# A first gated net with four plain tiles, quarter sums on POOL, and rotary angles moved to that net's last stretch

## The reference

```python
D_MODEL = 1024; SEQ = 512; DEPTH = 2; D_FF = 2816

def swiglu(h, w_gate, w_up, w_down):
    return (jax.nn.silu(h @ w_gate) * (h @ w_up)) @ w_down

def first_block(x, ...):
    for l in range(DEPTH):
        x = x + 0.5 * swiglu(rms_norm(x, ffn1_norm[l]), ffn1_wg[l], ffn1_wu[l], ffn1_wd[l])
        ...
        x = x + 0.5 * swiglu(rms_norm(x, ffn2_norm[l]), ffn2_wg[l], ffn2_wu[l], ffn2_wd[l])
    return rms_norm(x, final_norm)

def rope_tables(positions):
    half = QK_ROPE // 2
    inv_freq = ROPE_THETA ** (-jnp.arange(half, dtype=jnp.float32) / half)
    ang = positions.astype(jnp.float32)[..., None] * inv_freq
    return jnp.cos(ang), jnp.sin(ang)
```

## Time and profile before

| | before |
|---|---|
| median of 3 runs | 2509.74 us |
| the profiled execution | 2509.46 us |
| its span (first to last instruction) | 2507.7 us |
| around the span | 1.8 us |
| PE busy | 2492.7 us, 99% of the span |
| DVE busy | 1959.6 us, 78% |
| ACT busy | 1229.5 us, 49% |
| POOL busy | 305.2 us, 12% |
| granted TensorE clock | 1.00 (2.4 GHz) over the span |

### The profile page before, as it was taken

One profiled execution on the slowest core, in us unless ns is written; L12 is line 12 of the kernel. 1 busy time (PEld: TensorE's weight loads), 2 busy tenths in 40 slices (PEclk: granted clock), 3 DMA queues, 4 the chain that ended last, 5 costly groups with the idle time before them and its releaser, 6 DMA issues.

```text
span 2507.7 us, 37031 instructions
## 1 busy us (share of the span) xinstructions
PE 2492.7 (99%) x14550; PEld 2204.2 (88%) x14550; DVE 1959.6 (78%) x2788; ACT 1229.5 (49%) x1957; POOL 305.2 (12%) x250
## 2 busy tenths in 40 slices
PE   8999999999999999999999999999999999999998
PEld 7999988889999889999888899998888888899997
DVE  7878867778888688887777888876899786876663
ACT  6444444444444454444553544445577535644442
POOL 4000001320000000000023100000186221200002
PEclk9999999999999999999999999999999999999999
DMA  5333342223333423333323233334333333233331
GB/s 157 99 97 101 98 107 83 82 87 99 95 110 100 118 79 104 96 108 112 101 65 96 74 101 107 101 106 136 88 72 82 123 92 113 83 108 99 99 100 59
DMA packets 487299, 246.87 MB, mean 98 GB/s; under 512 B 42321, under 2 KB 483926, under 8 KB 486870
## 3 DMA queue, kind: packets, MB, share of 16 engines
q1 hardware_dynamic: 486674, 244.19, 33.9%
q10 hardware_dynamic: 452, 0.32, 0.1%
HBM read 240.27 MB, written 4.19 MB: 97 GB/s over the span
## 4 chain that ended last, share of the span: by engine, by line
PE 95%; DVE 3%; ACT 1%; issue 0%; DMA 0%; POOL 0%; DVEq 0%
PE bank L878 8%; PE bank L877 8%; PE bank L876 8%; PE bank L764 6%; PE bank L766 6%; PE bank L765 6%; PE psS L898 4%; PE psS L899 4%; PE psS L900 4%; PE psT L942 2%; PE psT L943 2%; PE psT L944 2%; PE psT L764 2%; PE psT L766 2%; PE psT L765 2%; PE bank L1441 1%
## 5 line engine op out<-in xcount | busy, mean ns | idle before, releaser
L2238 DVE TENSOR_TENSOR wlo<-raw,whi 128x1024 fp32r<-128x1024 f32 (+2 forms) x212 | 289.3, 1366 | 51.6 <-ACT whi L1567 48.4
L764 PE MATMUL bank<-xhi,whi 128*128 128x512 f32 x672 | 265.3, 395 | 0.0
L765 PE MATMUL bank<-xlo,whi 128*128 128x512 f32 x672 | 261.9, 390 | 0.0
L766 PE MATMUL bank<-xhi,wlo 128*128 128x512 f32 x672 | 261.8, 390 | 0.0
L876 PE MATMUL bank<-xsh,whi 128*128 128x256 f32 x840 | 237.8, 283 | 0.0
L877 PE MATMUL bank<-xsl,whi 128*128 128x256 f32 x840 | 237.7, 283 | 0.0
L878 PE MATMUL bank<-xsh,wlo 128*128 128x256 f32 x840 | 237.7, 283 | 0.0
L1567 ACT ACTIVATE whi<-raw 128x1024 fp32r<-128x1024 f32 (+2 forms) x209 | 214.5, 1030 | 46.0 <-PE bank L766 22.5
L2297 DVE TENSOR_TENSOR wlo<-tw,whi 128x1024 fp32r<-128x1024 f32 x140 | 171.6, 1225 | 62.2 <-ACT whi L1603 62.0
L898 PE MATMUL psS<-hhi,whi 128*128 128x512 f32 x488 | 191.7, 393 | 0.0
L899 PE MATMUL psS<-hlo,whi 128*128 128x512 f32 x488 | 191.6, 393 | 0.0
(11 more groups left out here) (701 smaller groups left out, 7275.0 us busy)
## 6 DMA issues: line engine op xcount, KB each, us to landing
raw<-in_ffn_wg SPq DMA_DIRECT2D x88, 512.0 KB
raw<-in_ffn_wu SPq DMA_DIRECT2D x88, 512.0 KB
raw<-in_w_in SPq DMA_DIRECT2D x53, 512.0 KB
raw<-in_w_mlp SPq DMA_DIRECT2D x40, 512.0 KB
raw<-in_ffn_wd SPq DMA_DIRECT2D x48, 256.0 KB
raw<-in_ffn_wd SPq DMA_DIRECT2D x24, 448.0 KB
raw<-in_ffn_wd SPq DMA_DIRECT2D x48, 192.0 KB
raw<-in_ffn_wd SPq DMA_DIRECT2D x48, 128.0 KB
```

The source lines that it names most:

```text
L764: pe.matmul(dest, a, rhs_hi(k), start=start and k == 0, stop=False)
L765: pe.matmul(dest, a, rhs_lo(k), start=False, stop=False)
L766: mm = pe.matmul(dest, b_, rhs_hi(k), start=False, stop=stop and k == tiles - 1)
L2238: dve.tensor_tensor(wlo[:, a:a + n], raw[:, a:a + n], whi[:, a:a + n].bitcast(F32), ALU.subtract).then_inc(s_split, 1)
```

## The change

Net 0 gets two pairs like the other nets: four plain tiles, 18 windows, another cut of the down-projection. In net 0 the quarter sums are taken from DVE's queue and written into POOL's, where the angles stood; there each group waits for ACT's copies and for the low half of the group before. DVE's low half of the quarter sums stands in net 0 after the SiLU product of its tile and no longer ahead of the up product. The angles follow behind the sums on POOL, from the moment at which the last stretch of net 0 has added its first tile to `x`; they use `inv6` and `first_inv` as scratch, and the wait for them ahead of weight sums stands in net 1.

```diff
-    PLAINS = (3, 2, 2, 2)
+    PLAINS = (2, 2, 2, 2)
...
                 def weight_sums(j):
                     c, g = c0 + 4 * (PLAIN + j), G0 + j
                     landing(c + 1)
-                    if j == 0:
+                    if j == 0 and nf == 1:
                         dve.wait_ge(s_ro, 13)
...
                 def quarter_sums(i):
+                    if nf == 0:
+                        return
...
-                        if 2 * j + p in QUARTERS_AT:
+                        if nf and 2 * j + p in QUARTERS_AT:
                             quarters_lo(QUARTERS_AT[2 * j + p])
                         dve.wait_ge(s_used, c + 2 * p + 2)
                         dve.tensor_tensor(tmp[2 + p][:, :], b(up_b[p][:, :]), inv[:, :], ALU.mult).then_inc(s_us, 1)
                         dve.wait_ge(s_us, f + p + 1)
                         dve.wait_ge(s_si, f + p + 1)
                         dve.tensor_tensor(tmp[2 + p][:, :], tmp[2 + p][:, :], tmp[p][:, :], ALU.mult).then_inc(s_h, 1)
+                        if not nf and 2 * j + p in QUARTERS_AT:
+                            quarters_lo(QUARTERS_AT[2 * j + p])
...
-            r, n = rope[64:128, :], sqt[64:128, :]
+            near, far, half = xg2[:, 0:S], xg2[:, S:2 * S], (slice(0, QT), slice(QT, S))
+            s1, s2, s3, s4 = (xsum[:, j * QT:(j + 1) * QT] for j in range(4))
+            for i in range(4):
+                pool.wait_ge(k_xg, i + 1)
+                if i:
+                    pool.wait_ge(k_xl, i)
+                pool.tensor_tensor(s1, near[:, half[1]], far[:, half[1]], ALU.add).then_inc(k_xs, 1)
+                pool.tensor_tensor(s3, near[:, half[0]], near[:, half[1]], ALU.subtract).then_inc(k_xs, 1)
+                pool.wait_ge(k_xs, 4 * i + 1)
+                pool.tensor_tensor(s2, s1, near[:, half[0]], ALU.subtract).then_inc(k_xs, 1)
+                pool.wait_ge(k_xs, 4 * i + 3)
+                pool.tensor_tensor(s4, far[:, half[0]], s2, ALU.subtract).then_inc(k_xs, 1)
+            r, n, part_r = rope[64:128, :], inv6[64:128, :], first_inv[64:128, :]
...
-            pool.wait_ge(s_inv, 1)
+            pool.wait_ge(s_x, KC + 1)
...
-                pool.tensor_scalar(acc[64:128, :], n, -cst, None, ALU.mult).then_inc(s_ro, 1)
+                pool.tensor_scalar(part_r, n, -cst, None, ALU.mult).then_inc(s_ro, 1)
```

More of the change, by code:

```diff
@@ L3275, in _ @@
                 pool.wait_ge(s_ro, step)
-                pool.tensor_scalar(acc[64:128, :], n, -cst, None, ALU.mult).then_inc(s_ro, 1)
+                pool.tensor_scalar(part_r, n, -cst, None, ALU.mult).then_inc(s_ro, 1)
                 pool.wait_ge(s_ro, step + 1)
-                pool.tensor_tensor(r, r, acc[64:128, :], ALU.add).then_inc(s_ro, 1)
+                pool.tensor_tensor(r, r, part_r, ALU.add).then_inc(s_ro, 1)
                 step += 2
@@ L3281, in _ @@
             pool.tensor_scalar(r, r, 3.1415925, -3.1415925, ALU.min, ALU.max).then_inc(s_ro, 1)
-            c, nn = rope[64:96, :], sqt[64:96, :]
+            c, nn = rope[64:96, :], inv6[64:96, :]
             pool.wait_ge(s_ro, 10)
```

## The result

| | before | after |
|---|---|---|
| median of 15 runs each | 2509.66 us | 2514.59 us |
| the profiled execution | 2509.46 us | 2514.59 us |
| its span | 2507.7 us | 2512.7 us |

What follows compares the result with a forecast made beforehand. PE, busy 99% of the span, was taken as the bound, so only its work or stops count. -1.53 (work) + 4.8 (stop) + 0 (angles) = +3.3 us on 2509.74 gave 2513.0 us, range 2509.4 to 2515.0.

Steps and rivals of the forecast that it cites:

- the forecast proper: Whole kernel: 2513.0 us, band 2511.9 to 2514.5, given a chance of 0.62.
- less work on PE: Net 0: two plain tiles go, 21.76 us, against 20.23 us for more fast tiles and the down-projection's other cut; -1.53 us.
- start of the first window: Net 0's first window would start at 57.50 instead of 79.26, since two plain tiles go.
- walk of DVE without meetings: Plain tiles of net 0: DVE's fourth low half ends at 61.6, PE wants it at 60.4; a stop of 1.2 us.
- meetings of POOL and DVE: Plain tiles of net 0: POOL's sums and DVE's two-SBUF operations hold each other up, adding 3.6 us to the stop.
- both together: the stop: PE's stop at the third product of net 0's first window: 1.2 + 3.6 = 4.8 us (3.7 to 5.7), paid once.
- angles in the last stretch: Net 0's last stretch: the angles on POOL cost 0, at most 0.6 us, as DVE has spare time each round.
- A sum of 0.74: Price of one 256-column quarter sum on POOL: 0.74 us, between 0.65 and 0.83.
- The places of the meetings: Norm's last step, a unit of weights, corner weights through weight sums, last corner's rest: 1.5, 0.5, 1.3 and 0.3 us.
- under 0.9 a round: Net 0's last stretch: the angles hold DVE less than the 0.9 us it has to spare in each round.
- the slower rival: Net 0's last stretch: angles hold DVE for whole rows, rounds grow to about 6, PE loses some 5 us; 2518; chance 0.09.
- The up product and the SiLU product, now ahead of the low half: DVE's walk in net 0's plain tiles: having them ahead of the low half makes 1.3 us of the 1.2 us stop.

Runs made afterwards that it cites:

- fills: Changed kernel with each net 0 quarter sum on POOL replaced by a constant fill that reads nothing, leaving those sums out; 2509.31 us.
- the filled run: Changed kernel with 18 extra matmuls of 512 columns on PE, results unread, ahead of the third product of net 0's first window; 2512.94 us.
- the angles alone: Kernel before with only the rotary angles moved on POOL to net 0's last stretch; three pairs and sums on DVE as before; 2513.28 us.
- sums on DVE: Changed kernel with net 0's quarter sums on DVE instead of POOL, each group behind DVE's own low half of the group before; 2512.90 us.
- low half first: Changed kernel with the quarter sums' low half back ahead of the up product in all four tiles of net 0; 2520.51 us.
- three edits: Changed kernel with down-projection's first share before the third product, fourth group's sums on DVE, last tile's low half before up product, corner rest behind SiLU product; 2514.81 us.
- side first: Changed kernel with the down-projection's first share (9 matmuls) moved ahead of the third product of net 0's first window; 2514.25 us, in two groups.
- fourth group on DVE: Changed kernel with the fourth group of quarter sums on DVE and, in the last plain tile, their low half ahead of the up product; 2512.52 us.

## Why the prediction was right, and where it was short

It put the time at 2513.0 and the sign right; 1.6 us were missing. The median lies 0.09 above the band that was the forecast proper (to 2514.5), and inside the range because that went on to 2515.0. By the profile's steps the changed kernel's loss is:

| step of the prediction | forecast, us | measured, us |
|---|---|---|
| less work on PE | -1.53 | first window to stage behind 308.28; without stop and clock 302.27, net 1 has 302.28 |
| start of the first window | 57.50 | 57.69, +0.19 |
| walk of DVE without meetings | +1.2 | 0.87 with fills, which are shorter than sums |
| meetings of POOL and DVE | +3.6 | 3.55 between fills and sums, at most 0.4 of it length |
| both together: the stop | +4.8 | 4.47 |
| angles in the last stretch | 0 | no stop between units; some 0.2 at the stage behind |
| TensorE's clock behind the stop | not named | +1.54 by rows, 1.65 by the filled run |

-1.53 + 0.19 + 4.47 + 0.2 + 1.54 = 4.9, the measured 4.93. The 0.19 is there ahead of the plain tiles already (DVE's row at 25.00 before is at 25.18 after); no run shows why. The 0.2 lies where the stage behind net 0 waits for the last halves of its input; before has no such wait, and each kernel with the late angles has one (0.17 with fills, 0.8 with the angles alone).

- **The gain and the stop** were read rightly. Third product "near 65": 65.02. A sum of 0.74: 0.73 to 0.75 where nothing meets it. The places of the meetings are the four that were named, and the sizes 1.5, 0.5, 1.3 and 0.3 measured 1.25, 0.42, 1.35 and 0.53.
- **The step that was missing** is in the sum: a stop was priced at its length, with no term and no rival for the clock behind it. The prediction read PE's speed from a kernel whose PE does not rest from 36 to 85 us, and so took 0.12 us a matmul also for what follows a rest of 4.5.
- **The angles**: the answer of 0 was nearly right, but by luck. The hold "under 0.9 a round" was 0.9 to 1.9 us in three rounds, because three of the four additions met a two-SBUF operation of DVE and held it 0.9 to 1.1 us each; a scalar operation held 0.3 to 0.4 (at 346.05 and 353.97), near the 0.5 that was taken. The rounds grew to 5.7, nearly the 6 of the slower rival. What saved the stretch is the longer unit that the same change brings, and the lead of 1.4 us that DVE had gained on it, which neither the forecast nor the rival's price had counted; 0.1 us of it was left. The stretch also had 29 us to go and not 33 when the angles began. Alone, the move costs 3.6 us.
- **"The up product and the SiLU product, now ahead of the low half, are 1.3 us of this"** holds of the last tile alone; over all four the new order saves 5.

## What to carry to other kernels

Price a new stop of PE at its length plus what the clock may take behind it, and look at the granted clock there before looking for a second cause; a few useless matmuls in the stop tell the two apart. Before work moves to POOL, look at what DVE has beside it: here 16 small sums that met DVE's two-SBUF operations made the third product 1.5 us later than on DVE itself. Work that fills one stop may have covered another, so look at what stood behind its old place.

## What the runs showed of the hardware

- TensorE's granted clock, behind rests of PE in this window (profiled executions): 0.50 from 65.0 to 68.4 behind 4.5 us; behind 3.0 us (sums on DVE) first 0.8 us of matmuls at full level and then 0.50 from 64.3 to 67.6; behind 9.8 us (low half first) 0.50 from 65.2, while PE still stood, to 75.5. Behind 3.2 us (three edits) it fell 1.1 us into the work, behind 2.4 us (side first) 1.3 us into it, behind 2.6 us (fourth group on DVE) not at all. So the length of the rest alone does not decide; what does stays open.
- A fill of POOL beside DVE's two-SBUF operations stretched none of them (31.16: 0.69 us, 45.81: 1.23); a sum stretched each that it met in the plain tiles by 0.4 to 0.5 us (0.69 to 1.10 and 1.17, 1.23 to 1.62 and 1.75).
